# Key-value boundary in token blocks with the value tiles first; the last norm in blocks with its weights on GpSimd

## The reference, cut to what matters

```python
x = x + short_conv_mixer(rmsnorm(x, mix_norm[0]), a_w_in[0], a_conv[0], a_w_out[0])   # stage "a"
x = x + conv_ffn(rmsnorm(x, ffn_norm[0]), ffn_up[0], ffn_conv[0], ffn_down[0])        # stage "f0"
kv = nsa_shared_kv(rmsnorm(x, kv_norm), w_kv, cmp_pe, cmp_w1, cmp_b1, cmp_w2)         # stage "b"
x = x + nsa_mixer(rmsnorm(x, mix_norm[1]), b_w_qg[0], b_w_o[0], kv, rel_bias)         # stage "b"
x = x + conv_ffn(rmsnorm(x, ffn_norm[1]), ffn_up[1], ffn_conv[1], ffn_down[1])        # stage "f1"
return rmsnorm(x, final_norm)                                                         # "end"

def conv_ffn(h, w_up, conv_w, w_down):     # w_up: 1024 x 5632, conv over 3 tokens, w_down: 2816 x 1024
    u = causal_dwconv(h @ w_up, conv_w)
    a, g = jnp.split(u, 2, axis=-1)
    return (jax.nn.silu(a) * g) @ w_down
```

## Time and profile before

| | us |
|---|---|
| median of three runs (622.99 to 626.23) | 625.33 |
| the profiled execution's own time | 623.39 |
| its span, first to last instruction | 621.6 |
| TensorE busy in the span | 607.8 |
| VectorE busy | 483.6 |
| ScalarE busy | 389.5 |
| GpSimd busy | 64.5 |
| mean granted TensorE clock, share of full speed | 0.999 |

### The profile page before, as it was taken

The page is one execution under the profiler, slowest core; times in us unless marked ns, Lnnn a source line. Parts: engine busy times, 40 slices in busy tenths (PEclk is TensorE's granted clock), DMA queues, the critical chain, the costliest instruction groups (busy, mean ns, idle before and its releaser), DMA issues.

```text
span 621.6 us, 11325 instructions
## 1 busy us (share of the span) xinstructions
PE 607.8 (98%) x3750; PEld 532.3 (86%) x3750; DVE 483.6 (78%) x946; ACT 389.5 (63%) x717; POOL 64.5 (10%) x82
## 2 busy tenths in 40 slices
PE   8999999999999999999999899999999999999995
PEld 8999997888888888888989777777988888888884
DVE  4888756888888877777887799938688888887765
ACT  7546337666666666668556488727766666666644
POOL 0110011000000000012131156610100000000010
PEclk9999999999999999999999999999999999999999
DMA  8796432555555555771376401033355555555521
GB/s 334 286 341 241 176 137 100 201 205 203 202 202 203 182 190 175 289 247 35 130 249 209 138 2 35 1 103 135 123 197 204 208 197 204 203 203 190 198 102 67
DMA packets 30353, 109.55 MB, mean 176 GB/s; under 512 B 3388, under 2 KB 3660, under 8 KB 30189
## 3 DMA queue, kind: packets, MB, share of 16 engines
q1 hardware_dynamic: 29756, 106.97, 48.6%
q0 software_dynamic: 560, 2.12, 1.0%
HBM read 108.01 MB, written 1.07 MB: 175 GB/s over the span
## 4 chain that ended last, share of the span: by engine, by line
PE 89%; DVE 5%; ACT 3%; issue 1%; DMA 1%; POOL 0%; DVEq 0%; ACTq 0%
PE bank L1241 24%; PE bank L1245 13%; PE bank L1190 10%; PE bank L1191 10%; PE bank L1192 10%; PE bank L1209 9%; PE bank L1214 4%; DVE w_lo L811 1%; PE bank L1556 1%; PE bank L1286 1%; ACT work L555 1%; PE bank L1588 1%; PE bank L1581 1%; PE bank L1221 1%; PE bank L1299 1%
## 5 line engine op out<-in xcount | busy, mean ns | idle before, releaser
L811 DVE TENSOR_TENSOR w_lo<-staged,w_hi 128x1024 fp32r<-128x1024 f32 x188 | 233.1, 1248 | 45.4 <-ACT w_hi L551 45.3
L551 ACT ACTIVATE w_hi<-staged 128x1024 fp32r<-128x1024 f32 x196 | 198.9, 1046 | 24.9 <-PE bank L1192 7.1
L1241 PE MATMUL bank<-gx,w_hi 128*128 128x512 f32 x656 | 163.3, 391 | 0.0
L1241 PEld LDWEIGHTS bank<-gx,w_hi 128*128 128x128 f32 x656 | 120.4, 188 | 23.4 <-DVE work L947 0.2
L1245 PEld LDWEIGHTS bank<-gx,w_lo 128*128 128x128 f32 x656 | 89.5, 190 | 6.4
L1245 PE MATMUL bank<-gx,w_lo 128*128 128x256 f32 x656 | 91.5, 282 | 0.0
L1190 PE MATMUL bank<-w_hi,y 128*128 128x512 f32 x208 | 81.5, 392 | 0.0
L1191 PE MATMUL bank<-w_lo,y 128*128 128x512 f32 x208 | 81.5, 392 | 0.0
L1192 PE MATMUL bank<-w_hi,y 128*128 128x512 f32 x208 | 80.9, 389 | 0.0
L680 ACT ACTIVATE work<-work,params 128x256 f32<-128x256 f32 x96 | 44.2, 504 | 54.1 <-DVE work L947 39.2
L694 ACT ACTIVATE y<-work 128x256 fp32r<-128x256 f32 x52 | 21.7, 418 | 77.6 <-DVE work L968 59.7
(11 more groups left out here) (186 smaller groups left out, 807.7 us busy)
## 6 DMA issues: line engine op xcount, KB each, us to landing
staged<-in_f_up SPq DMA_DIRECT2D x88, 512.0 KB, 5.2
staged<-in_f_down SPq DMA_DIRECT2D x44, 512.0 KB, 3.6
staged<-in_a_up SPq DMA_DIRECT2D x24, 512.0 KB, 7.2
staged<-in_b_up SPq DMA_DIRECT2D x24, 512.0 KB, 4.3
staged<-in_a_down SPq DMA_DIRECT2D x8, 512.0 KB, 3.7
staged<-in_b_down SPq DMA_DIRECT2D x8, 512.0 KB, 4.3
bias<-bias_rows POOLq DMA_DIRECT2D x1, 2048.0 KB, 12.1
x<-in_xt SPq DMA_DIRECT2D x1, 1024.0 KB, 9.4
```

Of the source, the lines that this page charges most:

```text
L551: nc.scalar.activation(w_hi[:, q["slot"], 0:n], staged[:, s, 0:n], ACT.Copy).then_inc(hi, 1)
L811: nc.vector.tensor_tensor(w_lo[:, q["slot"], 0:n], staged[:, s, 0:n], w_hi[:, q["slot"], 0:n].bitcast(F32), ALU.subtract).then_inc(lo, 1)
L1241: nc.tensor.matmul(dst, w_hi[:, s, kt * P:kt * P + P], gx[:, kt, :], start=kt == 0, stop=False, skip_group_check=True)
```

## The change

The key-value boundary uses `norm_halves`; `B_ORDER` begins with the value tiles, whose products are made for the first 128 tokens (`values(0)`, with the transposes of the other half ahead of its last tile) and then for the others (`values(1)`). The value products move from banks 4 and 5 to banks 0 and 1, other banks follow. The second set of high and low parts, `gq_hi` and `gq_lo`, follows both halves. The ten products of ones leave this boundary. In f0 and f1 the last unit goes through `last_step`, the half with the silu ahead of the other, with the split of its down tile behind the first read; the last two down shares are interleaved by block (`last_downs`), so that the first block is complete twelve products before the last one. The compressed inputs' shifts and high parts move behind the value tiles in ScalarE's order. `ends_T` and `vc` get 128 rows, of which the added ones are zero (a third memset on GpSimd), and the last product of `attend` is made once for each head on 64 columns. At the end GpSimd multiplies x by the norm's weights for three of four blocks as they come (`gained`), the first root is taken after two squares, VectorE multiplies two blocks by the root, ScalarE one, which it stores over its own queue, and VectorE makes the fourth as before.

```diff
-B_ORDER = ([("cmp", t) for t in range(4)] + [("key", t) for t in range(4)] + [("val", t) for t in range(4)]
+B_ORDER = ([("val", t) for t in range(4)] + [("cmp", t) for t in range(4)] + [("key", t) for t in range(4)]
...
-        vc = sb("vc", [2 * 32, 2, 2 * HD])
+        vc = sb("vc", [P, 2, 2 * HD])
...
+        xg = part(4400, 2 * D).rearrange("p (t d) -> p t d", t=2)
...
-        ends_T = part(P0 + 2 * HW, T, 2 * 32)
+        ends_T = part(P0 + 2 * HW, T)
...
-            return bank[b // 2 % 3][:, b % 2 * T:(b % 2 + 1) * T]
+            return bank[{2: 2, 3: 3, 4: 0, 5: 1}[b // 2]][:, b % 2 * T:(b % 2 + 1) * T]
...
-            return bank[{0: 1, 1: 0, 2: 2}.get(t, 7)][:, 0:T]
+            return bank[{0: 2, 1: 4, 2: 5}.get(t, 7)][:, 0:T]
...
+            for n, b in enumerate((0, 1, 3)):
+                sp.wait_ge(out_done, n + 1)
                 t, h = b // 2, slice(b % 2 * 512, b % 2 * 512 + 512)
-                sp.dma_start(out[:, t, h], x[:, t, h]).then_inc(stored, 16)
+                sp.dma_start(out[:, t, h], xg[:, t, h]).then_inc(stored, 16)
...
+            nc.gpsimd.memset(ends_T, 0.0).then_inc(zeroed, 1)
...
+            pool.wait_ge(final_landed, 16)
+            for b in range(3):
+                t, h = b // 2, slice(b % 2 * 512, b % 2 * 512 + 512)
+                pool.wait_ge(x_new, 4 * (NORM["end"] - 1) + b + 1)
+                nc.gpsimd.tensor_tensor(xg[:, t, h], x[:, t, h], final_row[:, h], ALU.mult).then_inc(gained, 1)
...
-                    if b == 2:
+                    if b == (1 if st == "end" else 2):
                         root(0)
                 root(1)
                 if st == "end":
+                    act.wait_ge(gained, 3)
+                    act.wait_ge(rstd_done, 2 * k + 1)
+                    nc.scalar.activation(xg[:, 1, 0:512], xg[:, 1, 0:512], ACT.Copy, scale=rstd_t[:, 1:2]).then_inc(third_done, 1)
+                    act.wait_ge(third_done, 1)
+                    act.dma_start(out[:, 1, 0:512], xg[:, 1, 0:512]).then_inc(stored, 16)
...
+            def last_step(st):
...
+                from_bank(0)
+                lead(st, "down", k, 0)
+                tapped_2(0)
+                from_bank(1)
+                act.wait_ge(convolved[st], 4 * k + 2)
+                nc.scalar.activation(conv[:, r, 0, :], conv[:, r, 0, :], ACT.Silu).then_inc(silued[st], 1)
+                tapped_2(1)
+                act.wait_ge(y_done[st], k + 1)
+                act.wait_ge(used_down, piece_of(st, "down", k, 0)["n"] - 2)
+                nc.scalar.activation(y_hi[:, r * T:(r + 1) * T], conv[:, r, 1, :], ACT.Copy).then_inc(y_hi_done[st], 1)
...
-                    step(st, FU - 2, (nxt[1:2], nxt[2:3], [(st, "down", FU - 1, 0)]))
-                    step(st, FU - 1, ([], [], nxt[3:]))
+                    step(st, FU - 2, (nxt[1:2], nxt[2:3], []))
+                    last_step(st)
+                    for q in nxt[3:]:
+                        lead(*q)
...
-            norm("b", meanwhile=B_PIECES(4, 6))
+            norm_halves("b", meanwhile=B_PIECES(4, 6))
...
-                if b in (2, 4):
-
-                    j = b // 2 - 1
+                if b in (6, 8):
+
+                    j = b // 2 - 3
                     act.wait_ge(b_evacuated, 2 * j + 2)
                     nc.scalar.activation(tokens[HD:P, j, :, 0:T - 1], tokens[0:HD, j, :, 1:T], ACT.Copy).then_inc(tokens_shifted, 1)
...
-                if b in (6, 12):
-                    j = 0 if b == 6 else 1
+                if b in (10, 12):
+                    j = 0 if b == 10 else 1
                     act.wait_ge(block_done, j + 1)
                     if j:
 
-                        act.wait_ge(used_up, UB + B_ORDER.index(("val", 3)) + 1)
+                        act.wait_ge(used_up, UB + B_ORDER.index(("key", 3)) + 1)
                     nc.scalar.activation(blocks[j][:, 0, :], block_in, ACT.Copy).then_inc(block_hi_done, 1)
                 if what == "val" and t == 3:
                     act.wait_ge(used_up, UB + b + 1)
                     for k in range(2):
-                        nc.scalar.activation(vals[:, k, :], bank[4 + k][:], ACT.Copy).then_inc(vals_done, 1)
+                        nc.scalar.activation(vals[:, k, :], bank[k][:], ACT.Copy).then_inc(vals_done, 1)
...
+            def norm_end():
+
+                for b in range(3):
+                    residual("end", b)
+                half("end", 0)
+                inverse("end", 0)
+                residual("end", 3)
+                for h in range(2):
+                    dve.wait_ge(gained, h + 1)
+                    cols = slice(h * 512, h * 512 + 512)
+                    nc.vector.tensor_scalar(xg[:, 0, cols], xg[:, 0, cols], rstd_t[:, 0:1], None, ALU.mult).then_inc(out_done, 1)
+                    if h == 0:
+                        half("end", 1)
+                inverse("end", 1)
+                nc.vector.scalar_tensor_tensor(xg[:, 1, 512:D], x[:, 1, 512:D], rstd_t[:, 1:2], final_row[:, 512:D],
+                                               ALU.mult, ALU.mult).then_inc(out_done, 1)
...
+            def last_step(st):
...
+                for c in range(2):
+                    dve.wait_ge(lo_read[st], k + 1 + c)
+                    nc.vector.tensor_tensor(shifted[:, r, c, 2:2 + T], bank[at + c][:, 0:T], shifted[:, r, c, 2:2 + T],
+                                            ALU.add).then_inc(scaled[st], 1)
+                    for n, which in enumerate((1, 0)):
+                        if n == 0:
+                            dve.wait_ge(tapped[st], 2 * k + c + 1)
+                        else:
+                            dve.wait_ge(convolved[st], 4 * k + 2 * c + 1)
+                        nc.vector.scalar_tensor_tensor(conv[:, r, c, :], shifted[:, r, c, which:which + T], tap(st, c, 0, k, which),
+                                                       conv[:, r, c, :], ALU.mult, ALU.add).then_inc(convolved[st], 1)
+                dve.wait_ge(convolved[st], 4 * k + 4)
+                dve.wait_ge(silued[st], k + 1)
+                nc.vector.tensor_tensor(conv[:, r, 1, :], conv[:, r, 0, :], conv[:, r, 1, :], ALU.mult).then_inc(y_done[st], 1)
+                dve.wait_ge(y_hi_done[st], k + 1)
+                nc.vector.tensor_tensor(y_lo[:, r * T:(r + 1) * T], conv[:, r, 1, :], y_hi[:, r * T:(r + 1) * T].bitcast(F32),
+                                        ALU.subtract).then_inc(y_lo_done[st], 1)
...
-                    q = nc.vector.tensor_copy(ends_T, bank[5][0:2 * 32, T:2 * T])
+                    q = nc.vector.tensor_copy(ends_T[0:2 * 32, :], bank[5][0:2 * 32, T:2 * T])
...
-            def cmp_pair(j):
...
+            def values(tt):
+
+                for t in range(4):
+                    q = piece_of("b", "up", B_ORDER.index(("val", t)), 0)
                     pe.wait_ge(lo_up, q["n"] + 1)
-                for kt in range(KT):
-                    if j == 0:
-                        pe.wait_ge(gx_lo_done, 8 * NORM["b"] + kt + 1)
-                    for b, q in enumerate(todo):
-                        s = q["slot"]
-                        mm = three(pair_bank(2 * j + b), w_hi[:, s, kt * P:kt * P + P], w_lo[:, s, kt * P:kt * P + P], gx_hi[:, kt, :],
-                                   gx_lo[:, kt, :], b == 0 and kt == 0, kt == KT - 1)
-                        if kt == KT - 1:
-                            mm.then_inc(used_up, 1)
+                    if tt == 0 and t == 3:
+                        turn_half("b", 1)
+                    for kk in range(2):
+                        kt = 2 * t + kk
+                        pe.wait_ge(gx_lo_done, split_of("b", tt, kt))
+                        mm = three(bank[tt][:], gx_hi[:, kt, tt * P:tt * P + P], gx_lo[:, kt, tt * P:tt * P + P],
+                                   w_hi[:, q["slot"], kk * 512:kk * 512 + 512], w_lo[:, q["slot"], kk * 512:kk * 512 + 512],
+                                   kt == 0, kt == KT - 1)
+                    if tt == 1:
+                        mm.then_inc(used_up, 1)
...
+            def last_downs(st):
+
+                units = (FU - 2, FU - 1)
+                tiles = [piece_of(st, "down", k, 0) for k in units]
+
+                def part(n, t, h):
+                    at, s = units[n] % 3 * T + t * P, tiles[n]["slot"]
+                    ws = slice(h * 512, h * 512 + 512)
+                    return three(bank[ACC[st] + 2 * t + h], y_hi[:, at:at + P], y_lo[:, at:at + P], w_hi[:, s, ws], w_lo[:, s, ws],
+                                 False, n == 1)
+
+                for n in range(2):
+                    pe.wait_ge(y_lo_done[st], units[n] + 1)
+                    pe.wait_ge(lo_down, tiles[n]["n"] + 1)
+                    for h in range(2):
+                        mm = part(n, 0, h)
+                        if n == 1:
+                            mm.then_inc(acc_done, 1)
+                    if n == 0:
+                        part(0, 1, 0)
+                part(1, 1, 0).then_inc(acc_done, 1)
```

(29 more changed lines are left out.)

91 lines of the change are left out of this document (36 added, 55 removed).

## The result

The changed kernel takes 625.72 us (median of 20 runs, 624.51 to 626.84), the kernel before, run beside it, 623.82 (20 runs): a ratio of 1.0025 with a 95% interval of 1.0017 to 1.0034. It is slower by a quarter of a per cent, where 622.7 was forecast. That forecast stood on the median of three runs, 625.33; on the 623.82 of twenty runs the same gain of 2.65 would give 621.2. The profiled execution took 625.03, with a span of 623.2 against 621.6.

A forecast was written before the change was run, and what follows sets the result against it. TensorE, 89% of the last-ending chain, was taken to bound the kernel. Terms of 0, 0.45, 1.0 and 1.2 sum to 2.65 us, taken off the median 625.33: 622.7; range 620.0 to 625.0.

The forecast's parts named there:

- The last units: Last unit and shares of f0 and f1: halved, interleaved order costs 0, at most 0.68 us in each stage.
- eight 256-wide steps: Behind the last up product: these replace about ten steps of 0.43, about 0.86 us earlier.
- That just covers it: cost 0: Last unit: its steps' 0.86 us gain covers y being wanted 0.68 us earlier, so no cost.
- The boundary: Key-value boundary: 1.2 us net on TensorE shrinks to 0.45 at `compressed`; bounds -0.4 and 1.65.
- The split ends product: Attention: 0.19 us for each `attend` on the chain, counted as 1.0 in all; bounds 0.4 and 2.4.
- The end: Last norm: VectorE finishes at 617.95 instead of 619.17, a gain of 1.2 us; bounds 0.3 and 1.4.
- rival C: At the end VectorE's root multiplication waits for GpSimd, leaving a 0.3 us gain there: 623.6 us; chance 0.08.
- 350 ns for 256 elements is the pace of one element a cycle: At the end: argument that VectorE's root multiplication needn't wait for GpSimd, only two-input operations being stretched.
- the execution's span ends 2.43 behind that: At the end: the span finishes 2.43 us behind VectorE's last multiplication, at 619.17 before the change.
- B: Compression comes later still and VectorE sets the attention loop: boundary -0.4, loop 0.4, 624.1 us; chance 0.12.
- D: Without the products of ones at the key-value boundary, the clock falls to 1.2 GHz: up to 633.6 us; chance 0.05.

The follow-up runs named there:

- experiment 1: Changed kernel with the last down tiles' splits of f0 and f1 moved from GpSimd to VectorE: 624.31 us, ratio 1.0006 to the kernel before.
- experiment 2: Changed kernel with the last units and last shares of f0 and f1 as in the kernel before: 624.37 us, ratio 1.0010 to the kernel before.
- experiment 3: Changed kernel with the last norm and its stores as in the kernel before, without GpSimd: 624.58 us, ratio 1.0016 to the kernel before.
- experiment 5: The kernel of experiment 1 with both low parts of the blocks moved from GpSimd to VectorE: 621.25 us, ratio 0.9965 to the kernel before.
- experiment 9: The kernel before with only the blocks' two low parts moved to VectorE: 624.30 us, ratio 1.0005 to the kernel before.
- experiment 4: Changed kernel with one ends product for both heads, as in the kernel before: 626.27 us, ratio 1.0035 to the kernel before.
- experiment 10: The kernel of experiment 9 with the ends product split as in the change: 622.38 us, ratio 0.9976 to the kernel before.
- experiment 12: Experiment 5 and experiment 6 combined, with the square root's table loaded ahead of the fourth key-value tile's split: 621.83 us, ratio 0.9960 to the kernel before.
- experiment 6: The kernel of experiment 1 with an end without GpSimd and all stores on SyncE's queue: 623.63 us, ratio 0.9987 to the kernel before.
- experiment 8: Changed kernel with the ten products of ones put back ahead of the first transposes: 625.03 us, ratio 1.0027 to the kernel before.
- experiment 11: Experiment 5 and experiment 6 combined, with last units, last shares and GpSimd's last down split as before: 623.34 us, ratio 0.9986 to the kernel before.

## Why the prediction was wrong

It was made of four terms that save, together 2.65 us; the trace has a loss of 1.04. Term by term:

**The last units (0).** This is the step that failed: "The down tile's split moves behind one ScalarE read of about 0.4 and is still done, with GpSimd's 2.41 us, some 2 us ahead of its use." That is true of the tile and left out the neighbour: in its new place the split lies on VectorE's multiply-adds. Together with what the new order costs by itself, the loss is 1.31 in f0 and 0.72 in f1; 1.7 of these 2.0 are the split's, as experiment 1 shows, and experiment 2 takes back all of it. The prediction had the rule at hand, since it let two-input operations of GpSimd and VectorE exclude each other ahead of `compressed`, and didn't apply it where it counted "eight 256-wide steps". The 0.68 in each stage that was given as the most it could cost was too small, too. "That just covers it: cost 0" was short by the 0.33 of f0 that experiment 1 leaves, and by nothing in f1. The rest of the step held: the interleaving starts the boundary 0.65 earlier (0.68 was said), and the first store 0.68.

**The boundary (0.45).** Net it gave 2.31 - 1.12 - 1.22 = -0.03. The gross gain (2.3), the moved transposes (1.05, measured 1.12 with the low part's wait) and the mechanism (two stretched splits in place of one, the wait at `compressed` grown from 0.46 to 1.6 us in experiments 2 and 3) were as forecast. The size was off by 0.5, within its bounds: two splits stand behind GpSimd as said, but they cost 1.8 us each, where the one before cost 1.35 and 1.1 was added for the second. Experiments 5 and 9 show it from both sides: on VectorE the low parts give 1.6 us behind the new boundary and 0.4 behind the old one.

**The split ends product (1.0).** 0.98 + 0.19 = 1.17 us: 0.20 at each pair against 0.19. The loop, the first five intervals, gained 0.66 where 0.6 was counted, so VectorE took back about what was feared, most of it in one interval; the others gained 0.51 where 0.4 was counted. Right, in mechanism and in size, and shown by experiments 4 and 10.

**The end (1.2).** It lost 0.16, and against the old end with the same interleaving 0.45. Two steps failed. The first is what rival C weighed and set aside: "350 ns for 256 elements is the pace of one element a cycle". The fixed part was taken as 0.05 us without a row for it. L917 takes 472 ns for 512 elements, so 256 more cost 122 ns, and 0.23 of the 0.35 are fixed; at that pace VectorE does use what GpSimd holds, and L917 waits (1.46), as do the multiplications of experiment 12. The Trainium skill (SBUF — State Buffer, Who interferes with whom) says that the exclusive pair is used by two-input operations and by `tensor_scalar` in its two-port mode alike; the trace agrees, with 1.46 against 0.47 us and 1.36 against 0.88. The second step took the end to follow the last multiplication ("the execution's span ends 2.43 behind that"), but the stores are a stream of 3.0 us that the first store starts. Experiments 3 and 6 show that with the same first store the end is the same to 0.07, and experiment 2 that a later one moves it.

**The rivals.** C came true in its mechanism. B's price at the boundary (-0.4) was nearer than the forecast's. D's mechanism fell with the clock of 1.00 at the boundary and with experiment 8. No case had its loss in the last units, and a loss had a chance of 0.05: of three places where GpSimd gets work or has it moved, one was taken to be a cost.

Profile and medians lie close: of the 1.9 us between the medians, 1.6 are in the spans, 0.56 of them in the unchanged start. Runs whose mean clock was 0.997 or more: 6 of the changed kernel average 624.80 and 15 of the kernel before, in the set beside experiment 1, 623.66, a difference of 1.14, beside the trace's 1.04 without and 1.6 with the start.

## What to carry to other kernels

Before work is given to GpSimd or moved on it, list what VectorE does in exactly that window, and count every operation that reads two tiles from SBUF, and every fast `tensor_scalar`, as standing still until GpSimd is done. Here the second low part took 2.25 us on GpSimd and 1.15 on VectorE, and the kernel was faster with both low parts on VectorE, although VectorE sets the time of that very stretch. A gain ahead of a wait is worth what the engine behind the wait leaves of it, so look for that engine first. Where the stores take longer than the last instructions, as here, look at the first store: it set the end, not the last instruction.

## What the runs showed of the hardware

**Stores.** Four stores of 256 KB on one or two queues end 4.5 to 4.7 us behind the request of the first (0.85 until data move, 2.95 to 3.1 for the data, 0.75 at the end). In two profiles of fourteen (experiments 1 and 11) the last data trickled in, at 20 to 25 GB/s, and the end came 5.4 and 5.6 us behind the first request.

**The clock.** In five of the fourteen profiles TensorE's granted clock falls to 0.50 with TensorE busy all through: for 3.41 us in four of them, for 6.8 in the fifth (experiment 12), and always 12 to 13 us behind the first `w1` product, where products on 48 columns of the array and of 60 to 120 columns have gone before. Experiments 2 to 4 have the same code there and no such stretch. In the four it cost nothing, since VectorE sets that stretch; in experiment 12 it cost 3 us.

Runs with a low mean clock (under 0.997) are also the longer ones: 14 of 20 of the changed kernel average 625.99 against 624.80 for the others, and 12 of 27 of the kernel before 624.78 against 623.66. It isn't shown that this 1.1 to 1.2 us is the stretch above: in the changed kernel it would cost nothing at that place, and a mean of 0.996 comes without it too (experiment 11, whose profile has its low clock only at the end, behind the last product). What makes these runs longer stays open, and so does whether 14 of 20 is more than 12 of 27 for a reason.
